# One more buffer for expert weights, the smaller expert's down projection in two transfers, and a new order inside each expert pair

## The reference

```python
for l in range(DEPTH):                       # DEPTH = 2
    xn = rmsnorm(h, norm_mix[l])
    ...                                      # projection, three head groups
    h = h + jnp.dot(jnp.concatenate([o_nsa, o_conv, o_hgrn], axis=-1), w_out[l])
    h = h + cross_attention(rmsnorm(h, norm_cross[l]), rmsnorm(mem, norm_mem[l]), ...)
    h = h + hier_moe(rmsnorm(h, norm_ffn[l]), ...)
return rmsnorm(h, norm_final)
# hier_moe: 32 experts; a token goes to 2 of the 8 experts of its best group
gu = lax.ragged_dot(xs, w_gu, sizes)         # 1024 -> 2 x 512
ys = lax.ragged_dot(jax.nn.silu(g_) * u_, w_dn, sizes)   # 512 -> 1024
```

## Time and profile before

| what | value |
|---|---|
| median of 3 runs | 1358.72 us (1358.48 to 1359.0) |
| the profiled execution, its own time | 1357.6 us |
| its span, from first to last instruction | 1355.6 us |
| PE busy | 1214.8 us (90%) |
| DVE, ACT, POOL busy | 482.4, 244.9, 77.5 us |
| bytes moved | 455.28 MB, mean 336 GB/s |

### The profile page before, as it was taken

One profiled execution on the slowest core, in us unless ns is written; L12 is line 12 of the kernel. 1 busy time (PEld: TensorE's weight loads), 2 busy tenths in 40 slices (PEclk: granted clock), 3 DMA queues, 4 the chain that ended last, 5 costly groups with the idle time before them and its releaser, 6 DMA issues.

```text
span 1355.6 us, 26062 instructions
## 1 busy us (share of the span) xinstructions
PE 1214.8 (90%) x10680; PEld 720.0 (53%) x10680; DVE 482.4 (36%) x1096; ACT 244.9 (18%) x569; POOL 77.5 (6%) x104
## 2 busy tenths in 40 slices
PE   7999997998898898899899999979999899898995
PEld 6878664444444344344488885644444444343442
DVE  4276436322322232222243663352322232222323
ACT  3013223111111111111120222321111111111111
POOL 0221300100000000000031130000000000000000
PEclk9999997999999999999999999979999999899998
DMA  8331357999999999999944113889999999999993
GB/s 363 110 146 63 125 242 316 401 427 429 428 428 429 427 430 428 428 429 427 417 168 158 35 63 125 356 348 430 426 428 430 427 429 428 428 429 427 429 429 147
DMA packets 33268, 455.28 MB, mean 336 GB/s; under 512 B 3776, under 2 KB 4160, under 8 KB 5312
## 3 DMA queue, kind: packets, MB, share of 16 engines
q1 hardware_dynamic: 33216, 454.59, 80.0%
HBM read 453.53 MB, written 1.05 MB: 335 GB/s over the span
## 4 chain that ended last, share of the span: by engine, by line
PE 63%; DMA 28%; DVE 4%; issue 2%; ACT 2%; SPq 1%; DVEq 0%; ACTq 0%
PE bank L517 61%; DMA share<-in_w_dn 27%; DVE rest L1890 1%; PE bank L747 1%; PE bank L576 1%; ACT rest L1296 1%; SPq L393 1%; DMA share<-in_mem 1%; PE bank L1053 0%; DVE h L1510 0%; ACT streams L1209 0%; ACT rest L1209 0%; PE bank L525 0%; DVE share L1584 0%; PE bank L1045 0%
## 5 line engine op out<-in xcount | busy, mean ns | idle before, releaser
L517 PE MATMUL bank<-share,rest 128*32 128x512 f32 (+1 forms) x2432 | 274.7, 533 | 52.2 <-DMA share<-in_w_dn 38.2
L517 PE MATMUL bank<-dense,rest 128*32 128x256 f32 (+2 forms) x1824 | 187.2, 474 | 8.9 <-DMA share<-in_w_gu 5.9
L517 PEld LDWEIGHTS bank<-share,rest 128*32 128x32 f32 x2432 | 99.7, 114 | 152.5 <-issue 119.4
L517 PE MATMUL bank<-ring,rest 128*32 128x256 f32 (+1 forms) x1792 | 175.5, 479 | 2.8 <-DVE rest L1841 1.8
L517 PE MATMUL bank<-streams,dense 128*128 128x256 f32 (+2 forms) x992 | 166.2, 341 | 1.8 <-ACT streams L1140 1.8
L517 PEld LDWEIGHTS bank<-streams,dense 128*128 128x128 f32 (+1 forms) x992 | 144.3, 177 | 19.1 <-issue 3.5
L517 PE MATMUL bank<-rest 96*128 96x512 f32 (+1 forms) x288 | 122.0, 579 | 34.2 <-DVE rest L1890 34.2
L517 PEld LDWEIGHTS bank<-rest,xhat 128*128 128x128 f32 x1056 | 126.1, 196 | 42.7 <-issue 42.7
L517 PE MATMUL bank<-rest,xhat 128*128 128x96 f32 x1056 | 137.0, 284 | 2.6 <-DVE rest L1799 2.6
L517 PEld LDWEIGHTS bank<-dense,rest 128*32 128x32 f32 (+1 forms) x1824 | 68.2, 111 | 115.9 <-issue 85.6
L517 PEld LDWEIGHTS bank<-ring,rest 128*32 128x32 f32 x1792 | 62.8, 111 | 105.0 <-issue 82.1
(11 more groups left out here) (241 smaller groups left out, 970.8 us busy)
## 6 DMA issues: line engine op xcount, KB each, us to landing
share<-in_w_dn SPq DMA_DIRECT2D x64, 2048.0 KB, 18.6
ring<-in_w_gu SPq DMA_DIRECT2D x48, 2048.0 KB, 20.6
dense<-in_w_gu SPq DMA_DIRECT2D x48, 2048.0 KB, 23.8
share<-in_w_gu SPq DMA_DIRECT2D x24, 2048.0 KB, 21.5
dense<-in_w_units SPq DMA_DIRECT2D x18, 2048.0 KB, 9.4
streams<-in_w_gu SPq DMA_DIRECT2D x8, 2048.0 KB, 27.0
dense<-in_w_units SPq DMA_DIRECT2D x4, 1024.0 KB, 6.0
dense<-in_w_units SPq DMA_DIRECT2D x2, 1184.0 KB, 5.6
```

The source lines that it names most:

```text
L517: return pe.matmul(out_ap, lhsT=lhsT, rhs=rhs, start=start, stop=stop, skip_group_check=True)
```

## The change

- **Slots.** A new tile `spare` (2 MB) holds slot 3 of odd pairs in both layers. In the last layer `streams` holds their slot 4 in place of slot 3. That makes 10 and 11 slots. `spare` is filled behind unit 8 of the dense part.
- **First loads.** Slots 1, 3, 4 and 5 of pair 0 are loaded when the recurrence's output has left its bank and the attention's is full, ahead of the output projection; slot 2 and the odd pair's 0 and 1 after it. In the last layer the odd pair's slot 4 takes the place of its slot 3 at the end.
- **The queue.** Both layers use the same `LEADS`. The larger's down tile goes ahead of the smaller's (in the last layer a pair ahead, at the end of the turn). The smaller's down tile goes as two transfers of 1 MB, which report to two semaphores.
- **PE in a pair.** `hid` is turned right behind gate-up, the next gather's four pieces are spread over the gaps, columns of the down projection come ahead of its rows, and the rows wait for the second half of the smaller's tile only at k = 2. ACT and DVE follow that order.
- **Dense part.** The first cross-attention group's exponentials come ahead of the copies of the memory values on ACT; `xo0` is copied by ACT instead of DVE; of the last transposed tile (`zT3`) DVE now takes half, from a bank of its own (`zT4`).
- **The end.** One inverse root for both halves; DVE multiplies the second half by the gain beforehand, and ACT scales it while DVE scales the first.
- Events of several stages share semaphores, and `dynamic_dma_scratch_size=1024` is passed to the builder.

```diff
+LEADS = [4] * 3 + [3] * 3 + [2] * 3 + [1] * 3
...
+        spare = sb("spare", [P, 4096])
...
-            return dense[:, s, :] if s < 3 else eslot(s)
+            return dense[:, s, :] if s < 3 else spare[:, :] if s == 3 else eslot(s)
...
-            return streams[:, :, :].rearrange("p s c -> p (s c)") if s == 3 else odd_slot(s)
+            return streams[:, :, :].rearrange("p s c -> p (s c)") if s == 4 else odd_slot(s)
...
-            return s < 3 or l == DEPTH - 1 and s == 3
+            return s < 4 or l == DEPTH - 1 and s == 4
...
+                    if s == 5:
+                        sp.dma_start(dst[:, 0:2048], src[:, 0:2048]).then_inc(eloaded[s], 16)
+                        sp.dma_start(dst[:, 2048:4096], src[:, 2048:4096]).then_inc(late_down_of[l], 16)
...
-                for u in range(3, 12):
+                for u in range(3, 9):
                     load_unit(u)
+                load_of(3, 3, True)
+                for u in range(9, 12):
+                    load_unit(u)
+                wait_drained(sp, l, "av")
+                bank_full(sp, l, "o7")
+                alone(sp)
+                for s in (1, 3, 4, 5):
+                    load_of(s % 2, s)
                 bank_full(sp, l, "wo3")
                 alone(sp)
-                for s in range(1, 6):
-                    load_of(s % 2, s)
+                load_of(0, 2)
+                load_of(2, 0, True)
+                load_of(3, 1, True)
                 bank_full(sp, l, "memv")
                 alone(sp)
                 load_of(0, 0)
-
-                load_of(2, 0, True)
-                load_of(3, 1, True)
                 bank_full(sp, l, LAST_USE[11])
                 alone(sp)
                 load_of(2, 2, True)
-                ahead = int(odd_apart(l, 3))
+                ahead = int(odd_apart(l, 4))
                 if ahead:
                     ...
-                    load_of(3, 3, True)
+                    load_of(2, 4, True)
...
+                def large_down(t, odd, it):
+
+                    sp.wait_ge(efilled[4], it * 2 - 1)
+                    alone(sp)
+                    load_expert((t + ahead) % PAIRS, 4, odd != (ahead == 1))
+
                 def down(t, odd, it):
+                    if not ahead:
+                        large_down(t, odd, it)
                     sp.wait_ge(efilled[4], it * 2 - 1)
                     alone(sp)
                     load_expert(t % PAIRS, 5, odd)
-                    sp.wait_ge(efilled[5], it * 2 - 1)
-                    alone(sp)
-                    load_expert(t % PAIRS, 4, odd)
...
-                    gather(t + 1, 0)
+                    pe.wait_ge(edrained[2], it * 2 + 3)
+                    pe.wait_ge(edrained[6], it * 2 + 1)
+                    alone(pe)
+                    for k in range(4):
+                        pe.transpose(banks[6][:, k * HD:(k + 1) * HD], hid[UP, k * P:(k + 1) * P], ident[UP, UP])
+                    gather(t + 1, 0, 0, 1)
+                    pe.wait_ge(edrained[3], it * 2 + 3)
+                    alone(pe)
+                    for c in range(4, 6):
+                        ins = pe.transpose(banks[6][:, c * HD:(c + 1) * HD], hid[UP, c * P:(c + 1) * P], ident[UP, UP])
+                    ins.then_inc(efilled[6], 1)
+                    gather(t + 1, 0, 1, 2)
...
-                    for e in range(2):
-                        expert_loaded(pe, l, t, odd, 4 + e)
+                    expert_loaded(pe, l, t, odd, 4)
                     for k in range(4):
+                        ...                      # columns into bank 5
+                    ins.then_inc(efilled[5], 1)
+                    for k in range(4):
+                        if k == 0:
+                            expert_loaded(pe, l, t, odd, 5)
+                        if k == 2:
+                            pe.wait_ge(late_down_of[l], t * 16 + 16)
                         for n in range(2):
                             ...                  # rows into bank 4
                     ins.then_inc(efilled[4], 1)
-                    ...                          # columns into bank 5
+                    gather(t + 1, 0, 2, 4)
...
                 turned("y", G_CROSS, 1)
+                exps(NN)
                 bk = bank_full(act, l, "memv")
                 ...
                 bank_drained(ins, "memv")
-                exps(NN)
                 keep_queries(1)
                 keep_pT(NN)
+                bank_drained(drain("xo0", [(coT[:, :, 0:P], lambda b: two(b[:, 0:256]), 1.0)]), "xo0")
                 exps(NN + 1)
...
+                bk = bank_full(dve, l, "zT4")
+                bank_drained(V.tensor_tensor(xnT[:, 6:8, P:256], bk[:, 0:256].rearrange("p (d t) -> p d t", d=2),
+                                             bc(pcol(l, G_FFN + 6, 2).unsqueeze(2), 2, P), MUL), "zT4")
...
+            V.tensor_tensor(xhat[:, 1, :], h[:, 1, :], gain_row, MUL)
             for tt in range(2):
                 dve.wait_ge(ev(f"squares{tt}_final"), 1)
-                setup.link(inverse_root(setup.link, rs[:, tt:tt + 1], ssq[:, tt:tt + 1], 1.0 / D))
-                V.scalar_tensor_tensor(xhat[:, tt, :], h[:, tt, :], rs[:, tt:tt + 1], gain_row, MUL,
-                                       MUL).then_inc(ev("out_ready"), 1)
+            inverse_root(setup.link, rs, ssq, 1.0 / D).then_inc(ev("root_final"), 1)
+            dve.wait_ge(ev("root_final"), 1)
+            V.scalar_tensor_tensor(xhat[:, 0, :], h[:, 0, :], rs[:, 0:1], gain_row, MUL,
+                                   MUL).then_inc(ev("out0_ready"), 1)
```

More of the change, by code:

```diff
@@ L71 @@
 LEVELS_K = [f"kt{n}" for n in HALVES[1:] + [128]]
+STAGES = {f"{what}{tt}": [f"{what}{tt}_{stage}" for stage in stages] for what, stages in (
+    ("h", ("cross", "ffn")), ("squares", ("cross", "ffn")), ("rstd", ("cross", "ffn")),
+    ("xhat", ("mix", "cross", "ffn"))) for tt in range(2)}
+ORDERS = {"qt": LEVELS_Q, "kt": LEVELS_K} | STAGES
+ORDER_OF = {name: of for of, names in ORDERS.items() for name in names}
 STEPS_AHEAD = 12
-LEADS = [[3] * 4 + [2] * 4 + [1] * 4, [4] * 3 + [3] * 3 + [2] * 3 + [1] * 3]
+LEADS = [4] * 3 + [3] * 3 + [2] * 3 + [1] * 3
 def flat(ap):
@@ L283, in nth @@
         def nth(name, l):
[L284 to L286 removed]
+            if name in ORDER_OF:
+                order = ORDERS[ORDER_OF[name]]
+                return l * len(order) + order.index(name) + 1
             return l + 1
@@ L470, in turn @@
                     if lead == 1:
-                        if not ahead:
-                            other_rows(t, odd, it)
                         down(t, odd, it)
                     large_rows(t, odd, it)
-                    if lead >= 2 and not ahead:
-                        other_rows(t, odd, it)
                     if lead == 2:
@@ L497, in _ @@
                 it = sp.snap(odd_reg, min_val=1, max_val=MAXP * PAIRS)
-                if not ahead:
-                    other_rows(PAIRS - 1, True, it)
                 down(PAIRS - 1, True, it)
@@ L993, in _, with gather @@
                     wait_drained(pe, l, USES[b][-1])
-                def gather(n, b):
-                    if b == 0:
+                def gather(n, b, d0=0, d1=4):
+                    if b == 0 and d0 == 0:
                         pe.wait_ge(onehot_ready, n + 1)
-                    pe.wait_ge(edrained[b], n + 1)
-                    for d in range(4 * b, 4 * b + 4):
+                    if d0 == 0:
+                        pe.wait_ge(edrained[b], n + 1)
+                    for d in range(4 * b + d0, 4 * b + d1):
                         for tt in range(2):
@@ L1133, in norm, with turned @@
                         scale(stage)
-                def turned(prefix, gain, tt):
+                def turned(prefix, gain, tt, parts=4):
                     bk = bank_full(act, l, f"{prefix}T{2 * tt + 1}")
                     alone(act)
-                    for d in range(4):
+                    for d in range(parts):
                         ins = act.activation(xnT[:, 4 + d, tt * P:(tt + 1) * P], bk[:, d * P:(d + 1) * P],
@@ L1746, in _ @@
                 maxima(NN + 1)
-                bk = bank_full(dve, l, "xo0")
-                bank_drained(V.tensor_copy(coT[:, :, 0:P], two(bk[:, 0:256])), "xo0")
                 normalise(NN + 1)
```

78 lines of the change are left out of this document (36 added, 42 removed).

## The result

| kernel | median (range, runs) | ratio to before, 95% interval |
|---|---|---|
| before, on the same chip | 1358.86 us (4 runs) | |
| changed | 1342.78 us (1342.27 to 1346.91, 4 runs) | 0.9888 [0.9868, 0.9908] |
| changed, again, beside the experiments | 1343.15 us (1341.39 to 1344.49, 4 runs) | 0.9886 [0.9872, 0.9901] |

The change makes the kernel 16 us faster; 1341.0 was predicted, in a range of 1335 to 1349. The profiled execution of the first row is its slowest (1346.91), so the lines of after come from the second (span 1340.4 us), which is 1355.6 - 1340.4 = 15.2 us shorter than the profile of before.

A forecast was written before the change was run, and what follows sets the result against it. Weight transfers were taken to bound the expert parts. 9.8 (tiles) + 6.3 (tails) + 2.1 (dense) + 0.3 (end) - 0.8 (halves) = 17.7 us off the profiled execution, giving a median of 1341.0 us, range 1335 to 1349.

The forecast's parts named there:

- What bounds the kernel: Expert parts: first release, plus 4.9 us for each tile not loaded by then, plus PE's work behind the last landing.
- Rival (a): Expert parts: extra tiles give nothing, as PE's pace or another wait takes over; 1350.8 us (1346 to 1355), chance 0.13.
- One tile more ahead: Before each layer's first release: one more tile loaded saves 4.9 us a layer, 9.8 in all, bounds 0 and 9.8.
- makes room for the extra tile: First loads, begun at about 165 before the output projection's end: gives nothing by itself, but makes room for the tile.
- Rival (c): Layer 1's first turn: holes while SP stands at `down` give back the tiles' gain; 1356 to 1361 us, chance 0.04.
- Two transfers: Smaller's down tile in halves, expert pairs: 32 more issues cost 0.8 us of stream time.
- the near bound of 1.6: Lower bound on the halves' cost in the stream: at most 0.05 us a junction, 1.6 us for 32.
- Rival (b): Expert stream: halves pay in line, so slower; 1372 us at 1 us a pair, 1423 at 2.6; chance 0.05.
- Work behind the last landing: Last pair's down projection: starts before the landing, gains 2.4 us in layer 0, 3.9 in layer 1; together 6.3.
- The dense part: Cross-attention to router: earlier exponentials and split `zT3` copy save 1.05 us a layer, 2.1 in all, bounds 0 and 4.
- The end: Kernel's end: one root chain and parallel scalings, with stores then sharing the rate, gain 0.3 us, bounds -0.8 and 1.1.
- Rival (d): Whole kernel: tails at their full 3.6 and 5.3 us, dense parts at upper bounds; below 1335 us, chance 0.04.

The follow-up runs named there:

- the base: The changed kernel itself, against which the follow-up kernels were made: 1342.8 to 1343.2 us.
- the last run: Changed kernel plus five unused matmuls before the wait for chosen experts, gate-up columns ahead of rows in the second half, smaller's down tile whole: 1337.46 us, 0.984.

## Why the prediction was right, step by step

**What bounds the kernel.** Right, and the part of the working that carries the rest. Tiles behind the first release at the stream's pace set each layer's length. The old slots cost 4.77 and 4.96 us, where one tile was put at 4.9. Rival (a), tiles that give nothing, is out: it wanted that run within 3 us of the base, and it came 9 us over. The new pair order cost clock (0.95 in layer 0's stretch, against 0.98 before and 0.99 with the old order put back) and PE busy time (390 against 375 us), and the stretch covered that too.

**One tile more ahead.** Right: 9.7 us by the stretches, some 9 by the medians, 9.8 predicted. The sentence that the earlier start "makes room for the extra tile" was not needed: with the first loads at their old place the time is the same. Rival (c), a hole in layer 1's first turn, did not come: `down` was issued 16.5 us after the first release (16.3 foreseen), and the share stayed 1.01.

**Two transfers.** The term was too small: 2.1 to 2.9 us (0.07 to 0.097 a junction) by the kernels with the small tile whole and with all tiles in halves, against the 0.8 taken; the near bound of 1.6 was too low as well. That bound took 4.91 us a tile from a rate rounded to 1 GB/s and compared it with a stretch that had the landing in it; the stretches now show 418.11 / 84 and 413.12 / 83, some 4.98 us a tile, against 421.71 / 85 and 417.14 / 84, some 4.96. Rival (b), at 0.58 us a pair and more, was out by a factor of six to eight. The rule of the Trainium skill that spoke for it ("DMA: Bandwidth & Descriptors", section Bandwidth: 78% of the peak rate for 1 MB) does not show in a queue that is kept full: with all tiles in halves, 421 of 428 GB/s are left. (The estimate made from it was also summed wrongly: 2 x 20 us less the other terms' 18.5 is a loss of 21.5 us, not 24.)

**Work behind the last landing.** Right in size, 2.58 and 4.10 us against 2.4 and 3.9, and in what follows when. The last half lands at 665.3: the down projection starts 2.1 us ahead of that (663.22) and ends 3.3 us behind it, where 2 and some 3 were foreseen. In layer 1 it is 2.2 (1320.29) and 3.2. The run with the old pair order splits the gain of layer 0: 16.41 - 15.45 = 0.96 us for the wait that is gone (0.97 us for ACT has taken the place of 1.92 for the tile), 15.45 - 13.83 = 1.62 for the order of PE's work. In layer 1 the projection's 7.06 us, at a clock of 0.79, fell to 5.4 as well. What was wrong is the weight of the halves: with the columns first a whole tile is late by so little (0 and 0.26 us) that the whole time doesn't show it. They matter once PE's own path is shorter, as the last run showed with its wait of 1.41 us, and even there they cost about what they give.

**The dense part.** The gains ahead of the router are there in full, and are partly used up behind it. The first cross group's transposes start at 200.37 without a wait, where they waited 0.73 us for DVE. From the output projection's last part to the gather it is 62.17 to 62.27 us in both layers of the two kernels with the old dense part (before, dense part as before), and in the eight profiles with the new one and no added matmuls 61.08 to 61.34 in layer 0 and 61.07 to 61.47 in layer 1: about 1.0 and 1.1 us, where 1.05 was put. But the first rows took 4.94 to 5.20 us in the four old stretches and 5.36 to 6.12 in all sixteen new ones, 0.6 more on average. In the profile of after this left 0.07 us at layer 0's first release and 0.58 in layer 1, together 0.65 of 2.1; undoing the edits cost 1.03 us in its profile and 1.3 to 1.7 in the medians. I had treated the distance from router to first release as fixed. It isn't: the clock is low there, and the same 32 matmuls took 3.64 us where PE had been kept busy. Why they are slower behind the shorter dense part is open.

**The end.** 0.25 us against 0.3.

**The sum.** 9.7 - 2.1 (the stretches' 7.62 us: extra tiles by the run with the old slots, the rest being the halves, 1.97 by the run with the tile whole) + 6.7 + 0.65 + 0.25 = 15.2 us in the profile, against 17.7 predicted. Halves and the dense part were each some 1.4 us too good, the tails 0.4 too small. 16 us by the medians. Rival (d), below 1335, did not come. Undone one at a time, the slots (8.8 to 9.2), the pair order (2.2 to 2.5) and the dense part (1.3 to 1.7) account for 12.3 to 13.4 of the 16 us. The new order of the two down tiles, layer 0's `LEADS` and the end have no run to themselves, so the rest is placed by the profiles alone.

## What to carry to other kernels

Where a stream of weights never rests, count from its first release to the last consumer's end: here each tile loaded before it was worth one tile's time (4.77 and 4.96 us), and an earlier first release about as much as it came earlier (with five matmuls 1.31 and 2.83 us, the whole 3.4 to 3.7). Then look for what stands at both ends. Here it was PE at half clock behind a wait of 5 us, and PE's path behind the last gate-up tile, not the last transfer; five matmuls without use and a swap of rows and columns took another 6 us off (1336.84).

A kernel that takes a resource away must keep the order of everything else, or it measures two things, as the run without the spare slot did.

## What the runs showed of the hardware that was not expected

- In a queue that is kept full, a 1 MB transfer in place of half a 2 MB one costs 0.07 to 0.10 us: 421 against 428 GB/s with all tiles cut in two, at a DMA share of 1.01 either way.
- Behind PE's wait of 5.15 us the granted clock was 0.50, 1.2 GHz. Sixteen gather matmuls took 3.70 us there, and 2.00 with PE busy ahead of them (1.00, that is 2.4 GHz).
- The same wait does not always have the same result. Behind 2.42 us of waiting for slot 3, the rows ran with 1.06 us a matmul in one profile of the changed kernel and with 0.59 in the other; with five added matmuls the first rows of layer 1 took 3.64 us in all three profiles, behind waits of 1.89 us, and those of layer 0 5.72, 5.34 and 3.64 us, behind 1.92, 2.18 and 2.18 us. What decides it is open.
- A float32 matmul of 128x512 with a 128x128 operand stands in the trace as two instructions of 0.44 us each (8.83 us for twenty, at a granted clock of 1.00).
